# Feed-forward layers in two phases: all gate and up chunks first, then the down projection by pairs of output tiles

## What is computed

```python
def swiglu(h, wg, wu, wd):
    return (jax.nn.silu(h @ wg) * (h @ wu)) @ wd      # wg, wu: 1024 x 2816, wd: 2816 x 1024
x = x + factor * swiglu(norm(x), wg, wu, wd)
```

## Time and profile before

| | |
|---|---|
| median of three runs | 1555.29 us |
| profiled execution, its time | 1554.21 us |
| its span, first to last instruction | 1552.4 us |
| busy share: PE, PEld, DVE, ACT | 98%, 90%, 77%, 52% |
| moved from and to HBM | 341 MB, 220 GB/s |
| chain that ended last | PE 84%, DVE 8%, ACT 5% |

### The profile page before, as it was taken

How to read it: one execution, slowest core, us unless ns; L and a number is a source line. 1 busy time by engine, 2 the same in 40 slices (tenths; PEclk the granted TensorE clock), 3 DMA queues, 4 the chain that set the end, 5 groups by cost and what they waited for, 6 DMA issues and landing times.

```text
span 1552.4 us, 27304 instructions
## 1 busy us (share of the span) xinstructions
PE 1514.0 (98%) x10698; PEld 1402.3 (90%) x10698; DVE 1202.0 (77%) x1491; ACT 812.4 (52%) x973; POOL 13.0 (1%) x33
## 2 busy tenths in 40 slices
PE   7999999899999999999999899999999999999998
PEld 6899999699999999999888899999999989999997
DVE  5898889968888868888867689889855566775555
ACT  6444454365444664444567664446644456564443
POOL 2000000000000000000000000000000000000000
PEclk9999999799999999999999999999999999999999
DMA  7998854158999459989453389986555554555551
GB/s 243 353 317 302 279 164 159 35 178 308 313 305 313 143 166 312 309 307 303 140 169 100 118 276 339 306 287 213 190 185 185 183 165 149 163 190 190 189 189 54
DMA packets 244730, 341.07 MB, mean 220 GB/s; under 512 B 5939, under 2 KB 188363, under 8 KB 244672
## 3 DMA queue, kind: packets, MB, share of 16 engines
q1 hardware_dynamic: 242704, 334.72, 64.6%
q0 software_dynamic: 1968, 5.54, 1.1%
HBM read 339.17 MB, written 2.63 MB: 220 GB/s over the span
## 4 chain that ended last, share of the span: by engine, by line
PE 84%; DVE 8%; ACT 5%; DMA 1%; issue 1%; SPq 0%; DVEq 0%; ACTq 0%
PE banks L1563 25%; PE banks L1564 13%; PE banks L1506 13%; PE banks L1508 13%; PE banks L1507 13%; DVE arena L1217 2%; ACT w_hi L479 2%; DVE w_lo L917 2%; PE banks L1697 1%; DMA ada<-in_ada_w 1%; ACT xn L494 1%; DVE xn L981 1%; ACT xs L512 1%; PE banks L1621 1%; PE banks L1529 1%
## 5 line engine op out<-in xcount | busy, mean ns | idle before, releaser
L917 DVE TENSOR_TENSOR w_lo<-raw,w_hi 128x2048 fp32r<-128x2048 f32 x244 | 557.3, 2286 | 112.9 <-ACT w_hi L479 112.9
L1563 PE MATMUL banks<-xs,w_hi 128*128 128x512 f32 x1728 | 609.1, 395 | 0.0
L479 ACT ACTIVATE w_hi<-raw 128x2048 fp32r<-128x2048 f32 x244 | 464.6, 1907 | 57.9 <-PE banks L1508 38.1
L1564 PE MATMUL banks<-xs,w_lo 128*128 128x256 f32 x1728 | 484.8, 281 | 0.0
L1563 PEld LDWEIGHTS banks<-xs,w_hi 128*128 128x128 f32 x1728 | 325.9, 189 | 74.4
L1564 PEld LDWEIGHTS banks<-xs,w_lo 128*128 128x128 f32 x1728 | 326.3, 189 | 0.0
L1506 PE MATMUL banks<-gu_hi,w_hi 128*128 128x256 f32 x960 | 272.2, 283 | 0.0
L1507 PE MATMUL banks<-gu_lo,w_hi 128*128 128x256 f32 x960 | 269.1, 280 | 0.0
L1508 PE MATMUL banks<-gu_hi,w_lo 128*128 128x256 f32 x960 | 269.0, 280 | 0.0
L1035 DVE SCALAR_TENSOR_TENSOR ada_acc<-ada,c_act,ada_acc 128x512 f32<-128x512 f32 x252 | 189.1, 750 | 7.7
L1506 PEld LDWEIGHTS banks<-gu_hi,w_hi 128*128 128x128 f32 x960 | 180.7, 188 | 2.2
(11 more groups left out here) (282 smaller groups left out, 2068.8 us busy)
## 6 DMA issues: line engine op xcount, KB each, us to landing
ada<-in_ada_w SPq DMA_DIRECT2D x72, 1024.0 KB, 5.5
raw<-in_ffn_wg SPq DMA_DIRECT2D x44, 1024.0 KB, 5.6
raw<-in_ffn_wu SPq DMA_DIRECT2D x44, 1024.0 KB, 5.3
raw<-in_ffn_wd SPq DMA_DIRECT2D x44, 1024.0 KB, 5.3
raw<-in_ffn_w_in SPq DMA_DIRECT2D x43, 1024.0 KB, 7.0
raw<-in_ffn_w_out SPq DMA_DIRECT2D x22, 1024.0 KB, 6.5
raw<-in_attn_w_qkv SPq DMA_DIRECT2D x12, 1024.0 KB, 5.1
raw<-in_w_in SPq DMA_DIRECT2D x10, 1024.0 KB, 5.3
```

The lines of the kernel that those rows point to most:

```text
L479: act.activation(w_hi[:, s, :], raw[:, s, :], ACT.Copy).then_inc(hi_ready, 1)
L917: dve.tensor_tensor(w_lo[:, s, :], raw[:, s, :], w_hi[:, s, :].bitcast(F32), ALU.subtract)\
L1563: pe.matmul(o, wh[:, k, m], pair[:, :, k, :], start=(k == 0), stop=False, skip_group_check=True)
L1564: ins = pe.matmul(o[:, 0:T], wl[:, k, m], pair[:, 0, k, :], start=False, stop=(k == KT - 1), skip_group_check=True)
```

## The change

A feed-forward gets 34 chunks (`FFN_CHUNKS`) and two phases, all written out (`Fori` is gone).

Phase one has 22 chunks (`GATED`), gate and up in turn. Their results rotate through three pairs of banks (`GATE_UP_AT`), and the split products go to `g_pair`, which keeps all 22 x 256 values in both parts; room for it is found by laying it over `cs_hi`, `cs_lo` and scratch. Phase two has 12 chunks: for each of four pairs of output tiles three chunks of 6, 8 and 8 row tiles of the down matrix, 256 columns wide (`ROWS`). Each weight tile now takes one matmul of 512 columns and one of 256 (`joined`). Output tiles have two halves, which `two_sided` adds to x one after the other, for a pair of tiles while the next pair is computed; the last two tiles are added on their own. The first chunks of a feed-forward use the same form, but for the first one or two.

The ada work of a block is spread by a table (`ADA_STEPS`) over chunks: ScalarE now makes the first of the eight products (`ada_product`) and the reduction (`ada_store`, four activations with an accumulator); VectorE makes the other seven. Two accumulators take turns. PE transposes a block two chunks after its last step (`turn`) and waits for the store of the block before, and ahead of phase two for the stores of all blocks turned in phase one.

Squares of the first six tiles are made and folded into one ahead of the end, so that the statistics take three matmuls instead of five (and three instead of eight for the second sum of a joined norm).

```diff
+ADA_FFN = 9 * D // ADA_W // 2
+ADA_PER = KT - 1
+GATED = 2 * STEPS
+ROWS = (6, 8, 8)
+FFN_CHUNKS = GATED + 4 * len(ROWS)
...
+ADA_STEPS = {a: 3 if a % 2 else 2 if a in (8, 14, 20) else 1 for a in range(3, GATED)}
+ADA_STEPS.update({23: 4, 24: 3, 26: 4, 27: 3, 29: 4, 30: 3})
+_slots = [a for a in sorted(ADA_STEPS) for _ in range(ADA_STEPS[a])]
+ADA_FROM, ADA_HALF, ADA_TO = ([_slots[ADA_PER * b + k] for b in range(ADA_FFN)] for k in (0, 2, ADA_PER - 1))
...
# sync
+                for i in range(FFN_CHUNKS):
+                    if i < GATED:
+                        load(c0 + i, over_k((gate, up)[i % 2], i // 2 * NC))
+                    else:
+                        pair, part = divmod(i - GATED, 3)
+                        k0 = sum(ROWS[:part]) * P
+                        w = down[k0:k0 + ROWS[part] * P, pair * NC:(pair + 1) * NC]
+                        load(c0 + i, w.rearrange("(k p) n -> p k n", p=P))
...
+                    for b in range(1, ADA_FFN):
+                        if ADA_HALF[b - 1] == i - 5:
+                            load_ada(f, b, 0)
+                        if ADA_TO[b - 1] == i - 5:
+                            load_ada(f, b, 1)
...
# scalar
+                def ada_product(b):
...
+                    act.activation(ada_acc[done % 2][:, :], ada[:, 0, 0:ADA_W], ACT.Identity, scale=c_act[:, 0:1],
+                                   bias=zero_col[:, :]).then_inc(ada_first, 1)
+                def ada_store(b):
...
+                    act.wait_ge(ada_summed, done + 1)
+                    for j in range(4):
+                        part = turn_bank(b)[:, j * P:(j + 1) * P]
+                        ins = act.activation(part, part, ACT.Copy, accum_out=mod[:, f // 2, at + j:at + j + 1])
+                    ins.then_inc(ada_stored, 1)
+                def ada_work(a):
+                    for b in range(ADA_FFN) if f < 4 else ():
+                        if ADA_TO[b] + 2 == a:
+                            ada_store(b)
+                        if ADA_FROM[b] - 1 == a:
+                            ada_product(b)
...
+                for a in range(2, GATED + 1):
+                    split(c0 + a + 2)
+                    if a % 2 == 0:
+                        if a > 2 or not d:
+                            up_low(a // 2 - 1)
+                        gu_high(a // 2 - 1)
+                    else:
+                        gate_low(a // 2)
+                        silu_of_sum(a // 2)
+                    ada_work(a)
...
# vector
+                for a in range(2, FFN_CHUNKS):
+                    if a == FFN_CHUNKS - 1 and f < 4:
+                        modulation(f // 2, f % 2)
+                    split(c0 + a + 2)
+                    if a <= GATED and a % 2 == 0:
+                        if a > 2 or not d:
+                            gu_mul(a // 2 - 1)
+                        ada_part(a)
+                        gu_low(a // 2 - 1)
+                    elif a <= GATED:
+                        gate_sum(a // 2)
+                        ada_part(a)
+                    else:
+                        pair, part = divmod(a - GATED, 3)
+                        if part == 0:
+                            two_sided((2 * pair - 2, 2 * pair - 1))
+                        if part == 2 and pair:
+                            early(pair - 1)
+                        ada_part(a)
...
+                fold(xn, sq_added, 3 * PAIRED_NO[nxt], sq_folded, 2 * AFTER_NO[nxt])
...
+                for k in (6, 7):
+                    two_sided((k,))
+                    if nd is not None:
+                        u_low(nd, k)
...
# tensor
+            def joined(o, s, k, nb, pair, first, last):
+                wh, wl = lin(s, w_hi), lin(s, w_lo)
+                m = slice(nb * P, (nb + 1) * P)
+                pe.matmul(o, wh[:, k, m], pair, start=first, stop=False, skip_group_check=True)
+                return pe.matmul(o[:, 0:T], wl[:, k, m], pair[:, 0, :], start=False, stop=last, skip_group_check=True)
...
+                for a in range(3 if n in DEFER else 1, GATED):
+                    turned(a)
+                    arrived(c0 + a)
+                    if a >= 3 and a % 2 == 0:
+                        pe.wait_ge(gu_ready, s0 + a // 2 - 1)
+                    elif a >= 3:
+                        pe.wait_ge(silu_done, s0 + a // 2)
+                    wide_joined(slot(a), GATE_UP_AT[a % 3], n, False)
...
+                if f < 4:
+                    pe.wait_ge(ada_stored, ADA_FFN * f + sum(at + 2 < GATED for at in ADA_TO))
+                for a in range(GATED, FFN_CHUNKS):
+                    pair, part = divmod(a - GATED, 3)
+                    turned(a)
+                    if pair == 3 and part == 0 and f < 4:
+                        pe.wait_ge(ada_stored, ADA_FFN * f + sum(at + 2 < FFN_CHUNKS - len(ROWS) for at in ADA_TO))
+                    arrived(c0 + a)
...
+                        ins = joined(banks8[:, DOWN_AT[pair] + nb, :], slot(a), r, nb, g_pair[:, :, k, :], k == 0,
+                                     k == 2 * STEPS - 1)
```

More of the change, by code:

```diff
@@ L349, in step @@
[L349 to L353, removed]
-                    load(cl + 2, over_f(down, (i + 1) * NC), i)
-                    if with_ada:
-                        ada_block(i, 1)
-                load(cl, over_k(gate, 2 * NC))
-                load(cl + 1, over_k(up, 2 * NC))
-                load(cl + 2, over_f(down, NC))
@@ L497, in plain_square, with u_high, early @@
                 act.activation(ub[:, k, :], x[:, k, :], ACT.Square).then_inc(ev("plain_sq"), 1)
+            def u_high(n, d, k):
+                scale, shift = norm_cols(d)
+                act.wait_ge(x_ready, 8 * (n - 1) + k + 1)
+                if k == 0 and shift is not None:
+                    act.activation(xs[:, 0, :, T:T + 2], shifts(d), ACT.Copy)
+                act.activation(xs_hi[:, k, :], x[:, k, :], ACT.Identity, scale=scale(k), bias=zero_col[:, :])\
+                    .then_inc(xhi_ready, 1)
+            def early(n, pair):
+                d, joint = deferred(n), n + 1 < len(STAGES) and JOINT[n + 1]
+                for k in (2 * pair, 2 * pair + 1):
+                    if d is not None:
+                        u_high(n, d, k)
+                    square(n, k)
+                    if joint:
+                        plain_square(k)
             def norm(n):
@@ L1046, in ffn, with fold @@
+                def fold(squares, added, at, folded, at_folded):
+                    for i in (1, 2):
+                        dve.wait_ge(added, at + i + 1)
+                        if i == 2:
+                            dve.wait_ge(folded, at_folded + 1)
+                        dve.tensor_tensor(squares[:, 0, :], squares[:, 0, :], squares[:, 2 * i, :], ALU.add)\
+                            .then_inc(folded, 1)
                 if n == 0:
@@ L1704, in ffn @@
[L1704 to L1706 removed]
+                if f < 4:
[6 more added lines that the diff above has]
+                    arrived(c0 + a)
+                    k0, rows = sum(ROWS[:part]), ROWS[part]
+                    last = a == FFN_CHUNKS - 1
+                    order = [(r, nb) for nb in range(2) for r in range(rows)] if last else \
+                        [(r, nb) for r in range(rows) for nb in range(2)]
+                    for r, nb in order:
+                        k = k0 + r
+                        if pair == 0 and nb == 0 and (k % 2 == 0):
+                            pe.wait_ge(gulo_ready, s0 + k // 2 + 1)
+                        ins = joined(banks8[:, DOWN_AT[pair] + nb, :], slot(a), r, nb, g_pair[:, :, k, :], k == 0,
+                                     k == 2 * STEPS - 1)
+                        if last and nb == 0 and r == rows - 1:
+                            ins.then_inc(tile_done, 1)
+                    ins.then_inc(chunks_done, 1)
```

621 lines of the change are left out of this document (294 added, 327 removed).

## The result

The changed kernel takes **1615.48 us** (median of 4 runs, 1614.34 to 1620.09), the kernel before on the same chip 1555.26 us (1554.26 to 1556.95). The ratio is 1.0392, 95% interval 1.0379 to 1.0405: slower by 60 us. Forecast were 1607 us and slower. The profiled execution took 1616.3 us; its span is 1614.5 us against 1552.4.

The account below looks back on a forecast made before the run. PE, by columns streamed, was taken to bound the kernel. From 1554.2 us: -1.0 (fewer matmuls) -3.0 (joined norm) +2.4 (feed-forward ends) +55 (handshake lag) = 1607.6, say 1607 us; 1585 to 1622 for this case, 1562 to 1625 for 8 in 10.

Parts of the forecast that it names:

- the case that was given 0.69: ScalarE/VectorE handshake lag makes PE late in the four ada feed-forwards: 1607 us, range 1585 to 1622, chance 0.69.
- the lag of 55 us: Four feed-forwards with ada work: PE late by 13.8 us in each, 122.7 us of chain against 108.9 of PE.
- Columns bind PE, fewer matmuls save 1.0 us: Down projection: 1056 fewer matmuls at equal columns, chunks 5.615 instead of 5.63 us, save 1.0 us over 66 chunks.
- The rule of 2.5 ns per matmul: Down projection: skill page's fixed cost per warm matmul; 1056 fewer would save 2.6 us, called of no weight.
- Joined norm, 3.0 us: Norm in front of the fifth feed-forward: 26 statistics records become 12, saving 14 x 0.216 = 3.0 us.
- Ends of feed-forwards, +2.4 us: Last products to Ln: folds and additions ahead of the last square make statistics 0.6 us later at four places.
- The handshake cycle, 11.65 us: Phase one: ScalarE/VectorE chain takes 11.65 us per two chunks against PE's 11.23, losing 0.42 us per pair.
- Store 1.65, product 0.52 us: Ada work on ScalarE in the first four feed-forwards: each store adds 1.65 us, each product 0.52, to the chain.
- Weights in 1 KB rows: Down weight loads: land in 5.6 us against 5.3 for 4 KB rows; asked for over 11 us ahead, costing nothing.
- What is late next: First four feed-forwards: PE waits 1 to 7 us before transposes and first down chunk; ScalarE's splits hardly wait for PE.
- The rival with 0.12: Lag plus falling clock after PE's wait before the down phase: half of 3 to 7 us, four times; 1614 to 1622, chance 0.12.

Follow-up runs that it names:

- the fastest variant, that of 1549.27 us: Changed kernel with ScalarE's store and next split both moved ahead, plus one ada step moved from chunk 20 to 22: 1549.27 us, ratio to before 0.9961.
- the run with the stores first: Changed kernel with only the ada store moved ahead of ScalarE's high split: 1610.53 us, ratio to before 1.0361.

## Why the prediction was right

The side, the mechanism, the place and nearly the size came out as written; 1615.5 lies in the range of the case that was given 0.69, though with the fall of the clock that was given to the other. That the total is so near is in part luck: the lag of 55 us was right with errors that met, and without the clock's 16 us the time would have been near 1600. Step by step:

- **Columns bind PE, fewer matmuls save 1.0 us.** Right in kind, the term was too small. I took the gate and up chunk's 5.615 us for the new down chunk. It takes 16 x 0.3466 = 5.55 us. The saving is 0.94 us per feed-forward, 5.6 in all, and 6.0 us as a whole kernel. I also left out the 224 matmuls fewer in first chunks, an estimated 1.2 us at 5.4 ns each. The rule of 2.5 ns per matmul (the Trainium skill, "TensorE: Matmul & The Clock Gate", "Wait — 56ns, not 53.3ns?"), which gave 2.6 us, was nearer than my 1.0; the trace has 5.4 ns.
- **Joined norm, 3.0 us.** Right: statistics of 5.4 us, from 1087.40 to the next product at 1092.82, became 2.4 us (1152.94 to 1155.34).
- **Ends of feed-forwards, +2.4 us.** Wrong: nothing was lost. From the first statistics matmul to Ln it was 3.3 us and is 1339.66 - 1336.74 = 2.9 us, but that matmul now starts 0.42 us behind the start of the last product (1336.32) and started 0.12 us behind it before. From the last product to Ln it is 3.34 us against 3.43 us. The folds end with PE's products (1336.59) and the four additions take 1.9 us, as I had them; square, statistics and hops behind them took 1.24 us (1338.42 to 1339.66), not 1.6. My own parts also add to 3.6 us, not to 3.9. At the four places together 0.2 us are saved.
- **The handshake cycle, 11.65 us.** 11.52 us: right within 1.1%. In the last feed-forward fifteen distances in a row are 11.52 or 11.53 us. Of the 0.13 us, 0.10 is the distance from sum to product, 0.72 us here (1459.72 to 1460.44 on VectorE) and 0.82 in the rows. PE has no wait for this chain in the last two feed-forwards, as said.
- **Store 1.65, product 0.52 us.** 1.13 and 0.70 us. The row of attention had activations 0.40 us apart, these are 0.28, as in the low bound. Per feed-forward this makes the term 5 x 0.34 = 1.7 us smaller, and the cycle 1.2 us smaller.
- **The late ada load, 2.4 us on the chain.** Not in the sum; it fills what the two terms above left. 13.8 - 1.7 - 1.2 + 2.4 = 13.3 us, and the trace has 14.0, 14.1, 13.0 and 11.8. The 55 us of the sum against 52.9 are thus right partly because errors met.
- **Weights in 1 KB rows.** I read 5.6 us to landing for them and 5.3 for 4 KB rows. Up weights, also in 1 KB rows, landed in 5.3 us before, and the new down chunks of 1 MB do too: the width of the rows made no difference that these medians show.
- **What is late next.** The waits of 0.3 to 3.7 us ahead of the turns and of up to 7.4 us ahead of phase two were forecast at "1 to 7", with these releasers. ScalarE's splits waited 0.8 us for PE in the first feed-forward from 30 to 154 us and not at all between 360 and 489: "next to no wait", as said.
- **The clock.** The rival with 0.12 came true beside the main case: 16 us of loss against the 7 to 15 us that I gave it. The four stretches behind the wait ahead of phase two cost 9.2 us, within my figure; what I left out is that waits ahead of the turns (of 1.8, 2.6 and 3.6 us) also had low clock behind them, 5.2 us in all, and the stretches at the start, 1.5 and 1.4 us. Those two do not come of the change: the kernel before has none there in its profiled execution, but the fastest variant, that of 1549.27 us, has low clock there as well.

The sum with measured terms: 1554.2 + 52.9 - 1.2 + 16 - 5.6 - 1.2 - 3.0 - 0.2 = 1611.9 against the profiled 1616.3. Of the missing 4.4 us, 1.4 are the second stretch of low clock near the start, and 1.5 a wait for a low split at the start of the fifth feed-forward (1168.44), which the kernel before has not; the rest stays open.

The experiments show the cause: a change of ScalarE's order alone takes 63 us off, more than the 60 us lost; doubling one product adds its length times five; taking the load's wait out gives most of its length; and the distances of the splits are the cycle plus what ScalarE does besides. The one run that seems to speak against it, the store on VectorE, gained nothing because waits for ada loads took its place on the cycle.

## What to carry to other kernels

When evictions of every chunk pass between two in-order engines, write down the closed cycle (split, split, sum, product, half) and compare it with PE's pace: in the last feed-forward's cycle of 11.52 us ScalarE was busy for 5.83 and VectorE for 7.17, and the pair was still slower than PE. Put the work that waits for nobody, here the next weight split, ahead of the work that waits for the other engine, and small stores that someone waits for ahead of both. A step taken off the busier engine is no gain if it lands on the closed cycle: ScalarE's store and product lengthened it by 1.13 and 0.70 us.

## What was not expected of the hardware

A matmul of 512 columns and one of 256 are followed by the next pair in 0.3466 us, three of 256 in 0.3520 us, with the same columns: 5.4 ns for each matmul. Idle times of PE of 1.8 us (between the starts at 83.35 and 85.44) and 2.6 us (121.59 and 124.46) differ in what follows: the first was followed by 3.4 us of clock at 0.50, the second by none; the idle time of 7.3 us was followed by 5.3 us of matmuls at 0.50. In the run with the stores first, waits of up to 3.5 us came often, and the clock fell three times in all the feed-forwards.
